# Two passes over the k tiles in the fp32r split-product steps of a three-block kernel

## What is computed

```python
def short_conv_mixer(h, w_in, conv_w, w_out):
    b_gate, c_gate, v = jnp.split(h @ w_in, 3, axis=-1)
...
    return (b_gate * u) @ w_out
...
def swiglu(h, w_gu, w_down):
    g, u = jnp.split(h @ w_gu, 2, axis=-1)
    return (jax.nn.silu(g) * u) @ w_down
...
    kv = (rms_norm(h, kv_norm) @ w_kv).reshape(bsz, seq, N_KV_SETS, N_KV_GROUPS, HEAD_DIM)
...
    qg = h @ w_qg
...
    return out @ w_o
...
    xin = h @ w_in
...
    return jnp.concatenate([attn, hm], axis=-1) @ w_out
```

## Time and profile before

| | us |
|---|---|
| median of three runs | 1001.1 (997.68 to 1001.53) |
| the profiled execution, its own time | 1000.11 |
| its span, from the first to the last instruction | 998.4 |
| PE busy (matmuls, 7886) | 965.8 |
| DVE busy | 711.4 |
| ACT busy | 486.0 |
| mean granted TensorE clock | 0.988 |

### The profile page before, as it was taken

How to read it: one execution, slowest core, us unless ns; L and a number is a source line. 1 busy time by engine, 2 the same in 40 slices (tenths; PEclk the granted TensorE clock), 3 DMA queues, 4 the chain that set the end, 5 groups by cost and what they waited for, 6 DMA issues and landing times.

```text
span 998.4 us, 19415 instructions
## 1 busy us (share of the span) xinstructions
PE 965.8 (97%) x7886; PEld 931.7 (93%) x7886; DVE 711.4 (71%) x1143; ACT 486.0 (49%) x709; POOL 81.3 (8%) x130
## 2 busy tenths in 40 slices
PE   8899999999999889889999999999999999999998
PEld 7899999999999768679999999999999899999998
DVE  5786777777768667967777777677986577665554
ACT  5343644444446426766434444345667565444441
POOL 6000001000000012330010000002000000000000
PEclk9999999999999989999999999989999999999999
DMA  9645857777745662025678686642543365564621
GB/s 273 218 166 189 268 167 261 267 262 242 277 164 157 205 237 85 2 88 204 194 230 300 231 292 234 207 127 85 169 126 129 128 211 193 188 225 154 204 90 42
DMA packets 131388, 186.99 MB, mean 187 GB/s; under 512 B 6272, under 2 KB 102656, under 8 KB 131328
## 3 DMA queue, kind: packets, MB, share of 16 engines
q1 hardware_dynamic: 123984, 159.82, 48.8%
q0 software_dynamic: 6912, 25.17, 7.4%
q10 hardware_dynamic: 432, 1.16, 0.4%
HBM read 185.09 MB, written 1.05 MB: 186 GB/s over the span
## 4 chain that ended last, share of the span: by engine, by line
PE 83%; DVE 9%; ACT 4%; issue 3%; DMA 1%; DVEq 0%; ACTq 0%
PE ps L1882 45%; PE ps L1960 15%; PE ps L1878 12%; PE ps L1880 3%; DVE ada_acc L1243 1%; DVE g_lo L1286 1%; ACT g_hi L737 1%; ACT g_hi L662 1%; PE ps L2074 1%; PE ps L2024 1%; DVE d_lo L1229 1%; DVE g_lo L1165 1%; PE ps L2137 1%; DMA xres<-in_x 1%; PE ps L1927 1%
## 5 line engine op out<-in xcount | busy, mean ns | idle before, releaser
L1882 PE MATMUL ps<-opa_hi,g_hi 128*128 128x256 f32 x864 | 250.3, 290 | 13.0 <-issue 8.4
L1882 PE MATMUL ps<-opa_lo,g_hi 128*128 128x256 f32 x864 | 247.6, 287 | 0.0
L1882 PE MATMUL ps<-opa_hi,g_lo 128*128 128x256 f32 x864 | 247.5, 286 | 0.0
L1882 PEld LDWEIGHTS ps<-opa_hi,g_hi 128*128 128x128 f32 x864 | 168.6, 195 | 16.3 <-issue 16.2
L1286 DVE TENSOR_TENSOR g_lo<-g_raw,g_hi 128x2048 fp32r<-128x2048 f32 x54 | 123.8, 2292 | 69.7 <-ACT g_hi L737 69.7
L1882 PEld LDWEIGHTS ps<-opa_lo,g_hi 128*128 128x128 f32 x864 | 168.5, 195 | 0.1
L1882 PEld LDWEIGHTS ps<-opa_hi,g_lo 128*128 128x128 f32 x864 | 168.4, 195 | 0.0
L1165 DVE TENSOR_TENSOR g_lo<-g_raw,g_hi 128x2048 fp32r<-128x2048 f32 x54 | 123.9, 2294 | 39.9 <-ACT g_hi L662 39.4
L1960 PE MATMUL ps<-hid_hi,d_hi 128*128 128x256 f32 x528 | 147.9, 280 | 0.1
L1960 PE MATMUL ps<-hid_hi,d_lo 128*128 128x256 f32 x528 | 147.5, 279 | 0.0
L1960 PE MATMUL ps<-hid_lo,d_hi 128*128 128x256 f32 x528 | 147.4, 279 | 0.0
(11 more groups left out here) (338 smaller groups left out, 1852.4 us busy)
## 6 DMA issues: line engine op xcount, KB each, us to landing
g_raw<-in_f_w_gu SPq DMA_DIRECT2D x44, 1024.0 KB, 8.7
ada_raw<-in_w_ada POOLq DMA_DIRECT2D x48, 512.0 KB, 5.8
d_raw<-in_f_w_down SPq DMA_DIRECT2D x22, 1024.0 KB, 5.1
g_raw<-in_w_in SPq DMA_DIRECT2D x14, 1024.0 KB, 7.9
g_raw<-in_w_gate SPq DMA_DIRECT2D x11, 1024.0 KB, 7.2
g_raw<-in_w_up SPq DMA_DIRECT2D x11, 1024.0 KB, 9.6
d_raw<-in_w_down SPq DMA_DIRECT2D x11, 1024.0 KB, 5.2
g_raw<-in_a_w_in SPq DMA_DIRECT2D x10, 1024.0 KB, 8.0
```

Of the source, the lines that this page charges most:

```text
L1882: mm = pe.matmul(pair(b)[:, a, :], wt[:, a * P:(a + 1) * P], xt, **st)
```

## The change

A `g_step` outside the feed-forward loops now runs over its k tiles twice. Two forms exist. With `late_lo` the head of the step waits for `g_hi_made` (and the PSUM bank) alone; the first pass issues hi·hi and hi·lo (32 matmuls, both with `w_hi`), then the engine waits for `g_lo_made`, and the second pass issues the 16 products with `w_lo`. With `hi_ready` the head waits for both weight parts as before; the first pass issues the products with the input's high part (hi·hi and `w_lo`·hi, 32 matmuls), waiting per tile for the high part, and the second pass the 16 products with the input's low part, waiting per tile for the low part.

`late_lo` is given to `CV` steps 2 to 7, all `BG`, `AO` 1 to 3, the second step of each feed-forward layer, `KV` 1 to 5, `WO` 2 and 3, and `MX` 1 to 13; `hi_ready` to `AO` 0, the first step of each feed-forward layer, `KV` 0 and `MX` 0. That makes 42 steps. `CV` 0 and 1, `QG`, `WO` 0 and 1, `MO` and the steps inside the feed-forward loops stay as they were. In `norm_parts` DVE now makes all eight tiles of `ybuf` before the first remainder.

```diff
@@ norm_parts
-                make_y(0)
-                make_y(1)
                 for k in range(KT):
-                    if k + 2 < KT:
-                        make_y(k + 2)
+                    make_y(k)
+                for k in range(KT):
                     dve.wait_ge(hi_signal, hi0 + k + 1)
@@ g_step
             if not waited and ks[0] == 0:
                 pe.wait_ge(g_hi_made, g + 1)
-                pe.wait_ge(g_lo_made, g + 1)
+                if not late_lo:
+                    pe.wait_ge(g_lo_made, g + 1)
                 if g >= 4:
                     g_free(g - 4)
-            for k in ks:
-                ready(k)
...
+            passes = ((0, 2), (1,)) if hi_ready else ((0, 1), (2,)) if late_lo else ((0, 1, 2),)
+            for i, products in enumerate(passes):
+                if late_lo and i == 1:
+                    pe.wait_ge(g_lo_made, g + 1)
+                for k in ks:
+                    if hi_ready and i == 0:
+                        hi_ready(k)
+                    elif hi_ready or i == 0:
+                        ready(k)
...
+                    sides = ((w_hi, hi), (w_hi, lo), (w_lo, hi))
+                    for a in range(2):
+                        for n in products:
+                            wt, xt = sides[n][0], sides[n][1][:, k, :]
+                            st = dict(start=(k == 0 and n == 0 and (a == 0 or g >= F2)),
+                                      stop=(k == KT - 1 and n == passes[-1][-1]), skip_group_check=True)
...
+        def a_hi_filled(fill):
+            return filled(opa_hi_made, 8 * A_FILL[fill])
@@ ffn
-            g_step(g0, hi, lo, ready)
+            g_step(g0, hi, lo, ready, hi_ready=hi_ready)
...
-            g_step(g0 + 1, hi, lo, no_wait)
+            g_step(g0 + 1, hi, lo, no_wait, late_lo=True)
@@ WO
             for s in (2, 3):
-                g_step(WO + s, opa_hi, opa_lo, no_wait)
+                if s == 2:
+                    pe.wait_ge(g_evac, evacs(WO))
+                g_step(WO + s, opa_hi, opa_lo, no_wait, late_lo=True)
```

More of the change, by code:

```diff
@@ L1856, in _, with g_step @@
     def _(pe):
-        def g_step(g, hi, lo, ready, tokens_out=False, waited=False, ks=range(KT), first_half=None, ahead=None):
+        def g_step(g, hi, lo, ready, tokens_out=False, waited=False, ks=range(KT), first_half=None, ahead=None,
+                   hi_ready=None, late_lo=False):
             slot = g % 2
@@ new lines, in g_step @@
+            passes = ((0, 2), (1,)) if hi_ready else ((0, 1), (2,)) if late_lo else ((0, 1, 2),)
[7 more added lines that the diff above has]
+                        ready(k)
+                    if first_half is not None:
+                        hi, lo = first_half if k < 4 else (opa_hi, opa_lo)
+                    w_hi, w_lo = (w[:, k, :] for w in ahead) if ahead else (w[:, slot, k, :] for w in (g_hi, g_lo))
+                    sides = ((w_hi, hi), (w_hi, lo), (w_lo, hi))
[4 more added lines that the diff above has]
+                                      stop=(k == KT - 1 and n == passes[-1][-1]), skip_group_check=True)
+                            if g >= F2:
+                                mm = pe.matmul(gate_and_up(g)[:, a, 0:T + 2], wt[:, a * P:(a + 1) * P], xt, **st)
+                            elif tokens_out:
+                                mm = pe.matmul(pair(b)[:, a, :], xt[:, a * P:(a + 1) * P], wt, **st)
+                            else:
+                                mm = pe.matmul(pair(b)[:, a, :], wt[:, a * P:(a + 1) * P], xt, **st)
@@ L1943, in both_squares, with ffn @@
             mm.then_inc(ss_done, 1)
-        def ffn(f, norm, hi, lo, ready):
+        def ffn(f, norm, hi, lo, ready, hi_ready):
             g0, d0 = FFNS[f], FT * f
-            g_step(g0, hi, lo, ready)
+            g_step(g0, hi, lo, ready, hi_ready=hi_ready)
             if f == 2:
                 sum_squares(norm)
-            g_step(g0 + 1, hi, lo, no_wait)
+            g_step(g0 + 1, hi, lo, no_wait, late_lo=True)
             if f < 2:
@@ L2005, in _ @@
         for s in range(8):
[L2006 removed]
+            g_step(CV + s, opa_hi, opa_lo, by_half(s) if s < 2 else no_wait, waited=s < 2, late_lo=s >= 2)
             if s == 1:
```

23 lines of the change are left out of this document (16 added, 7 removed).

## The result

The changed kernel takes 992.6 us (median of 5 runs, 990.9 to 994.7) against 1001.1 us (5 runs of the kernel before in the same session, 997.7 to 1001.5): a ratio of 0.9924, 95% interval 0.9900 to 0.9947, 7.6 us by the ratio and 8.5 us by the medians. Measured once more beside the experiments it takes 992.5 us against 999.2 us, ratio 0.9931 (0.9914 to 0.9949). The forecast was 993.2 us, 7.9 us less than before.

A forecast was written before the change was run, and what follows sets the result against it. The prediction took matmul count times pitch, plus interruptions, to bound the kernel. Its terms 3.58 + 1.70 + 0.90 + 1.28 + 0.4 = 7.9 us, taken from the 1001.1 us median, gave 993.2 us, range 989.5 to 997.5 us.

The forecast's parts named there:

- What bounds the kernel: Whole kernel: matmul count times pitch plus interruptions; the change acts only on interruptions, pitch effect 0, bounds 2.0 us either way.
- CV 4, 3.58 us: Convolution step 4: with the low part in the second pass, 3.42 us idle plus 0.16 us go, gaining 3.58 us.
- The half clock behind it, 1.70 us: Behind the CV 4 pause: the 3.40 us half-clock stretch goes with the idle, gaining 1.70 us, bounds 0 and 1.70.
- Feed-forward 0, WO and feed-forward 1, 2.2 us: Second feed-forward steps and WO 2: waits for low parts go, gaining 0.90 us in feed-forward 0, 1.28 in the others.
- KV 0 and 1, 0.4 us: First key-value steps: KV 0 ends 0.1 us earlier, KV 1 starts 0.3 us earlier, together 0.4 us.
- KV 4, counted at nothing: KV 4 starts 2.4 us earlier, matmuls get 4.1 us early, but QG 0's weight load takes it all: none counted.
- rival A: At QG 0: its load collides with the next 2 MB and lands 3.8 us late, giving 997.0 us; chance 0.09.
- The price of that idle, 0 with a bound of 1.15: QG 0 starts at half clock after longer idle; 2.25 us of later idle covers it, cost 0, or 1.15 us spill.
- rival C: Behind QG 0: the 6.80 us half-clock stretch from 367.30 shrinks, up to 3.4 us return, giving 989.8 us; chance 0.08.
- MX 0 and the other steps, 0: AO 0, first feed-forward steps, MX 0 and the other changed steps: no gain and no cost, 0.
- B: Behind the norms: DVE's lists eat the 0.90, 1.28 and 0.4 us and half clock spills, giving 997.0 us; chance 0.09.
- D: All changed steps: fresh weight tiles slow the pitch; from 6.4 ns per matmul the kernel is slower, 1006.1 us; chance 0.03.

The follow-up runs named there:

- The order alone: Changed kernel without its input passes, norm as before, late_lo steps in two passes but waiting for the low part at the head: 999.5 us, ratio 1.0005 to the kernel before.
- CV alone: Kernel before with only convolution steps CV 2 to 7 in two passes: 996.6 us, ratio 0.9974.
- without the input passes: Changed kernel without hi_ready in its six steps and with the norm parts in the old order: 993.2 us, ratio 0.9937 to the kernel before.
- KV alone: Kernel before with late_lo only in KV 1 to 5: 999.2 us, ratio 0.9999.
- the loads apart: Changed kernel with SP issuing the compression's value weights only after those of QG 0 and 1 have landed: 991.8 us, ratio 0.9931 to the kernel before.
- the pause filled: Kernel before with 12 small matmuls into an unused PSUM bank ahead of CV 4: 1001.5 us, ratio 1.0013.
- feed-forward and WO alone: Kernel before with late_lo only in the second step of each feed-forward layer and in WO 2 and 3: 997.6 us, ratio 0.9977.

## Why the prediction was right, and where its terms were off

**What bounds the kernel**: right. Only pauses moved; the pitch didn't. The order alone is worth 1.0005 (0.9995 to 1.0014), against bounds of plus or minus 2.0 us.

***CV 4, 3.58 us***: the mechanism was right and the size too large, about 2.4 us. The step that failed is taking the one profile's 3.42 us for the pause of a typical run. The end of the pause hangs on DVE's low part, and that execution made it 1.3 us late after a half-clock stretch at 12.3; the other five show 2.1 to 2.3 us.

***The half clock behind it, 1.70 us***: wrong as a term. The stretch is absent at its place in all seven profiles without the pause. But it didn't follow the pause in two of five others, and the mean clock of CV alone over all its runs is that of the kernel before. The Trainium skill's page "TensorE: Matmul & The Clock Gate", Part 1, has the throttled state as the default and activity as what releases it. That agrees with the seven profiles; it doesn't tell the three pauses from the two, or what the whole execution gets back.

***Feed-forward 0, WO and feed-forward 1, 2.2 us***: right as a sum, 1.9 to 2.3 us measured by themselves.

***KV 0 and 1, 0.4 us***: right by the traces, too small for the times. `KV` 0 gave 0.0 instead of 0.1, and `KV` 1 0.4 instead of 0.3: from the start of `KV` 0 to the next sum of squares it is 11.96 us before and 11.58 us without the input passes.

***KV 4, counted at nothing***: right, the sharpest test of it being KV alone with a ratio of 0.9999. `KV` 4's idle shrank by 2.4 us, as worked out (to 1.69 us), and the matmuls ahead of `QG` 0 are 11.6 us early where 7.8 come from before (the sum of squares in `KV`, 315.27 and 307.48): 3.8 for the 4.1 named. Then `QG` 0 takes it all back, and 1.25 us more: it is 6.5 us ahead, with 6.08 us of idle for about 5.1. The difference is the load, 9.2 us for 7.9, a term that the sum didn't have. The landing over 8 us after issue was named as a sign of being wrong by rival A; it came, and rival A's cause didn't hold.

***The price of that idle, 0 with a bound of 1.15***: the long stretch came, 6.8 us from 342.6, and the price was still 0. From `QG` 0 to the compression's output product it is 16.38 us now and 16.49 before: `QG` 0 was 6.54 us ahead, the output product is 6.65. The cover held. Of the 6.8 us only the 5.4 from 343.96 on lie on matmuls, at half clock 2.7 us lost, and the 2.25 us of idle ahead of the output product are used up by them; my bound had counted the whole stretch. Behind it the stretch of 6.8 us at 367.30, which rival C had in view, is gone, but two of 3.4 us at 376.2 and 413.8 are as long together, and nothing came back: 6.7 us ahead at the output product, 7.6 at the sum of squares in feed-forward 1, where `WO` and feed-forward 1 alone should add 1.3.

***MX 0 and the other steps, 0***: right; without the input passes the time is the same, 993.2 us.

The sum of the terms as the parts measured them is about 5 us, the whole 6.8 and 8.5 in two sessions (6.9 and 7.6 by the ratios). The forecast of 7.9 lies there, but not for all of its reasons, and in part by luck. It had 1.4 to 2.7 us too much at `CV` 4 (5.3, against 3.9 and 2.6 measured from the two sides) and lacked the 1.25 us of the late landing, and 2 to 3 us that no part shows by itself made up for that. The clock doesn't show as their source; they aren't settled, and the intervals are nearly as wide.

**The rivals.** A: a landing 1.3 us late, of its 3.8, was there and its cause wasn't; with the loads apart nothing changes. B: refuted by the feed-forward and `WO` parts. C: its stretch did go and two of half its length took its place. D: refuted.

## What to carry to other kernels

Where two parts of an operand are made one after the other, put the products with the later one last; here that cost nothing, and it brings the pause only where the next wait isn't already fixed by a load or another engine's list. Follow the chain of waits at the largest remaining pause before spending effort on the matmuls' side: a few lines moved on ACT and DVE brought about 5 us where the two passes had brought nothing. Take a pause's size from several profiles, and don't book the half clock behind it: a clock gain counts only if the mean granted clock over many runs rises.

## What the runs showed of the hardware

- The granted clock fell to half in stretches of 3.4, 6.8 and 10.2 us. Which pauses are followed by one differs between executions of nearly the same program (three of five at `CV` 4), while the mean over many runs stayed at 0.9880 to 0.9886 for the kernel before, CV alone, the order alone, the pause filled, and feed-forward and WO alone.
- A fetch of instructions of 0.02 MB took 1.07 us of one of the engines that carry the loads. Six loads of 2 MB with one in their tail were complete 1.3 us later than seven without; an eighth, early as those seven, had one too (the pause filled, 7.76 us), so the fetch alone doesn't decide it.
- Two loads of 2 MB issued 1.1 us apart on one queue didn't delay the first: 9.18 us with the second behind it, 9.02 alone.
- Products in another order run at the same pitch: in the changed kernel the chain from 35.93 has 201 matmuls in 24.12 us, 0.120 us each, as in an undisturbed step before (48 in 5.75 us). The order alone moved the time by a ratio of 1.0005 (0.9995 to 1.0014).
